# Reordering weight splits around the recurrence chains of a two-layer hybrid decoder, with eight more fill tiles in one wait

## What is computed

```python
p = x @ w_in                                  # (T, 6412): RWKV-7 | retention | mLSTM
o_rw  = rwkv7(...)                            # 8 heads of 64, matrix state, chunks of 128 tokens
o_ret = silu(gr) * rmsnorm(retention(q, k, v))      # 6 heads
o_ml  = sigmoid(om) * rmsnorm(mlstm(q, k, v, i, f)) # 6 heads
mix = concat([o_rw, o_ret, o_ml]) @ w_out
x1 = layernorm(ALPHA * x + mix)
x2 = layernorm(ALPHA * x1 + (silu(x1 @ w_gate) * (x1 @ w_up)) @ w_down)
```

## Time and profile before

| what | value |
|---|---|
| median of 3 runs | 2744.86 us (2743.68 to 2747.96) |
| the profiled execution, its own time | 2746.56 us |
| its span, from the first to the last instruction | 2744.8 us |
| TensorE busy | 2675.2 us, 97% |
| VectorE busy | 1624.7 us, 59% |
| ScalarE busy | 1163.2 us, 42% |
| granted TensorE clock, mean | 0.992 |
| HBM | 433.00 MB read, 162 GB/s |

### The profile page before, as it was taken

One profiled execution on the slowest core, in us unless ns is written; L12 is line 12 of the kernel. 1 busy time (PEld: TensorE's weight loads), 2 busy tenths in 40 slices (PEclk: granted clock), 3 DMA queues, 4 the chain that ended last, 5 costly groups with the idle time before them and its releaser, 6 DMA issues.

```text
span 2744.8 us, 55654 instructions
## 1 busy us (share of the span) xinstructions
PE 2675.2 (97%) x23551; PEld 2619.0 (95%) x23551; DVE 1624.7 (59%) x1768; ACT 1163.2 (42%) x1460; POOL 0.2 (0%) x4
## 2 busy tenths in 40 slices
PE   7999999999999999999999999999999999999997
PEld 7998899999999999999999998988999999999997
DVE  5567457788545455455586574577965555545444
ACT  4445343455333333333364453344643333333332
POOL 0000000000000000000000000000000000000000
PEclk9999999999999999999999999999999999999998
DMA  7644235366655666555565542353766665556653
GB/s 228 189 141 117 86 86 172 108 189 185 177 182 176 184 181 179 177 184 179 183 186 166 179 122 78 86 164 109 199 188 180 176 185 178 183 178 184 208 178 115
DMA packets 280774, 448.98 MB, mean 164 GB/s; under 512 B 45302, under 2 KB 76592, under 8 KB 280312
## 3 DMA queue, kind: packets, MB, share of 16 engines
q1 hardware_dynamic: 278984, 443.21, 54.2%
q10 hardware_dynamic: 1618, 3.24, 0.4%
HBM read 433.00 MB, written 11.78 MB: 162 GB/s over the span
## 4 chain that ended last, share of the span: by engine, by line
PE 87%; DVE 8%; ACT 2%; issue 2%; DMA 1%; ACTq 0%; SPq 0%; DVEq 0%
PE psum L705 19%; PE psum L707 19%; PE psum L706 19%; PE psum L738 6%; PE psum L739 5%; PE psum L740 5%; DVE w_lo L1756 2%; ACT w_hi L1323 1%; PE psum L728 1%; PE psum L729 1%; PE psum L730 1%; PE psum L937 1%; PE psum L1097 1%; PE psum L1082 1%; PE psum L1086 1%
## 5 line engine op out<-in xcount | busy, mean ns | idle before, releaser
L1752 DVE TENSOR_TENSOR w_lo<-w_raw,w_hi 128x1024 fp32r<-128x1024 f32 x496 | 606.1, 1225 | 680.6 <-ACT w_hi L1310 679.5
L1310 ACT ACTIVATE w_hi<-w_raw 128x1024 fp32r<-128x1024 f32 x504 | 533.7, 1060 | 887.0 <-PE psum L707 858.2
L705 PE MATMUL psum<-x_hi,w_lo 128*128 128x264 f32 (+3 forms) x3072 | 877.6, 286 | 2.3 <-DVE x_lo L2081 1.0
L706 PE MATMUL psum<-x_lo,w_hi 128*128 128x264 f32 (+3 forms) x3072 | 874.8, 285 | 0.0
L707 PE MATMUL psum<-x_hi,w_hi 128*128 128x264 f32 (+3 forms) x3072 | 874.3, 285 | 0.0
L705 PEld LDWEIGHTS psum<-x_hi,w_lo 128*128 128x128 f32 x3072 | 579.4, 189 | 3.5 <-issue 1.3
L706 PEld LDWEIGHTS psum<-x_lo,w_hi 128*128 128x128 f32 x3072 | 580.6, 189 | 0.2
L707 PEld LDWEIGHTS psum<-x_hi,w_hi 128*128 128x128 f32 x3072 | 579.5, 189 | 0.0
L1756 DVE TENSOR_TENSOR w_lo<-w_raw,w_hi 128x1024 fp32r<-128x1024 f32 x304 | 367.6, 1222 | 204.1 <-ACT w_hi L1323 187.7
L738 PE MATMUL psum<-x_hi,w_lo 128*128 128x264 f32 (+1 forms) x1376 | 412.0, 299 | 8.4 <-DVE w_lo L1756 5.2
L1323 ACT ACTIVATE w_hi<-w_raw 128x1024 fp32r<-128x1024 f32 x292 | 304.1, 1055 | 269.2 <-PE psum L740 164.8
(11 more groups left out here) (496 smaller groups left out, 2505.6 us busy)
## 6 DMA issues: line engine op xcount, KB each, us to landing
w_raw<-in_w_in SPq DMA_DIRECT2D x192, 512.0 KB, 4.2
w_raw<-in_w_gate SPq DMA_DIRECT2D x176, 512.0 KB, 3.8
w_raw<-in_w_up SPq DMA_DIRECT2D x176, 512.0 KB, 3.9
w_raw<-in_w_down SPq DMA_DIRECT2D x176, 512.0 KB, 3.7
w_raw<-in_w_out SPq DMA_DIRECT2D x64, 512.0 KB, 4.2
w_raw<-in_w_in SPq DMA_DIRECT2D x16, 262.0 KB, 2.8
r_sample<-in_state_ret SPq DMA_DIRECT2D x6, 512.0 KB, 7.7
out_s_ret<-r_sample SPq DMA_DIRECT2D x6, 512.0 KB, 6.2
```

Source lines behind the costliest of these rows:

```text
L705: mm(out, w1, bh[:, k, 0:nt], start=(k == 0), stop=False)
L706: mm(out, w0, bl[:, k, 0:nt], start=False, stop=False)
L1310: A(wh[:, j, :, :], raw[:, j, :, :], ACT.Copy).then_inc(S.hi_ready, 1)
L1752: TT(wl[:, j, :, :], raw[:, j, :, :], wh[:, j, :, :].bitcast(F32), ALU.subtract).then_inc(S.lo_ready, 1)
```

## The change

Five things change, all in the order of the instruction streams. (1) The first layer's plan has 45 instead of 37 tiles ahead of tok0, so that every later step of its RWKV part lies 8 tiles further on; the tiles come off those behind the last step. (2) Goals of the steps named in `waiting` are no longer two slabs behind TensorE: on ScalarE tok, pairs, more and l, on VectorE tok and l, in both chunks and both layers (`name[:-1]` takes the chunk's number off). (3) ScalarE's Tanh and Sigmoid of the gate inputs move from ahead of v0 to behind the squares at syt. (4) In the retention part VectorE makes one split ahead of the second pair, and the others of v1 and v2 behind the third. (5) The scans no longer take a split between them, and the splits of step kks move from ahead of the wait for the spread norm to behind L2222.

```diff
--- before.py
+++ after.py
@@ -474,7 +474,7 @@
     rw_last = [('sa', 16), ('sv', 7), ('sy', 17), ('gn', 5), ('gnss', 8), ('gnsp', 9)]
     rw_steps = [
         [('in', 0), ('a', 7), ('g', 7), ('kk', 11), ('kks', 9), ('bonus', 24)] +
-        chunk_steps(0, 37) + chunk_steps(1, 10) + rw_last,
+        chunk_steps(0, 45) + chunk_steps(1, 10) + rw_last,
         [('in', 0), ('a', 7), ('g', 7), ('kk', 11), ('kks', 9), ('v', 88), ('bonus', 6)] +
         chunk_steps(0, 28) + chunk_steps(1, 12) + rw_last]
     ml_steps = [('spread_m', 14), ('spread_e', 12), ('turn0', 18), ('turn1', 5), ('score', 5), ('num0', 9), ('num1', 7),
@@ -492,11 +492,12 @@
     class Parts:
 
 
-        def __init__(self, plan_, one, pos, slabs=GROUP_SLABS):
+        def __init__(self, plan_, one, pos, slabs=GROUP_SLABS, waiting=()):
             self.i, self.one, self.goals, before = 0, one, {}, 0
             at_ = lambda tile: slab_of(pos, slabs, tile)
             for name, n in plan_.items():
-                self.goals[name] = max(at_(before), at_(n) - 2, at_(max(n - 1, 0)) // slabs * slabs)
+                behind = 0 if name[:-1] in waiting else 2
+                self.goals[name] = max(at_(before), at_(n) - behind, at_(max(n - 1, 0)) // slabs * slabs)
                 before = n
             self.goals['end'] = at_(plan_['end'])
             self.names = list(self.goals)
@@ -1349,7 +1350,7 @@
                                 act.wait_ge(S.a_done, 3 * l + 1)
                             A(pml[:, 4 * (group - 8) + n, :], ps[:, n, 0:T], ACT.Copy).then_inc(S.bank_free, 1)
                     hi_in(l, 8 * pos + RING + i)
-                return Parts(plan_, one, pos)
+                return Parts(plan_, one, pos, waiting=('tok', 'pairs', 'more', 'l'))
 
 
             xp = a['x_prompt'][0].rearrange("(t p) d -> p t d", p=128)
@@ -1440,10 +1441,6 @@
                     bg.to(name)
                 act.wait_ge(S.a_kv_turned, n + 1)
                 A(kst[:, :, :].rearrange("p a k -> p (a k)"), ps[:, 4, 0:128 * AP_], ACT.Copy).then_inc(S.a_kv_ready, 1)
-                if not ml:
-                    act.wait_ge(S.rw_mix, l + 1)
-                    A(px[0:64, 12, 0:T], px[0:64, 12, 0:T], ACT.Tanh)
-                    A(px[:, 13, 0:T], px[:, 13, 0:T], ACT.Sigmoid).then_inc(S.rw_in, 1)
                 for name in tuple(f'v{p}' for p in range(AP_)) + ('sy',):
                     bg.to(name)
                 act.wait_ge(S.a_y_kept, 3 * n + 2)
@@ -1451,6 +1448,9 @@
                 bg.to('syt')
                 A(sq[:, 3:AH, 0:SEQ], ay[:, 3:AH, 0:SEQ], ACT.Square)
                 if not ml:
+                    act.wait_ge(S.rw_mix, l + 1)
+                    A(px[0:64, 12, 0:T], px[0:64, 12, 0:T], ACT.Tanh)
+                    A(px[:, 13, 0:T], px[:, 13, 0:T], ACT.Sigmoid).then_inc(S.rw_in, 1)
                     bg.to('sumsq')
                 act.wait_ge(S.a_y_ready, n + 1)
                 if ml:
@@ -1995,7 +1995,10 @@
                     carried()
                     dve.wait_ge(S.a_sample_loaded, 48 * (n + 1))
                 for p in range(AP_):
-                    bg.to(f'v{p}')
+                    if ml or p == 0:
+                        bg.to(f'v{p}')
+                    if not ml and p == 1:
+                        bg.step()
                     dve.wait_ge(S.a_vspread, n * AP_ + p + 1)
                     b0 = 4 if ml or p != 1 else 6
                     kv = ps[:, b0:b0 + 2, :].rearrange("p a (b v) -> p (a b) v", v=128)
@@ -2004,6 +2007,9 @@
                     else:
                         STT(sam[:, p, :, :], sam[:, p, :, :], gam[:, p:p + 1], kv, ALU.mult, ALU.add).then_inc(S.a_pair_done, 1)
                     dve.wait_ge(S.a_pair_done, n * AP_ + p + 1)
+                if not ml:
+                    bg.to('v1')
+                    bg.to('v2')
                 if ml:
                     carried()
                     dve.wait_ge(S.m_n_loaded, 48 * (l + 1))
@@ -2187,7 +2193,7 @@
                 attention(l, False, 2 * l, bg)
 
 
-                bg = Parts(rw_plan[l], lambda i: lo1(s0 + 8 * RW_POS + RING + i), RW_POS)
+                bg = Parts(rw_plan[l], lambda i: lo1(s0 + 8 * RW_POS + RING + i), RW_POS, waiting=('tok', 'l'))
                 then = (lambda ins: (own(ins), bg.step()))
                 dve.wait_ge(S.bank_free, freed(l, IN_ORDER.index(1)))
                 for i in range(5):
@@ -2200,7 +2206,7 @@
                 for b in range(4):
                     for c in range(NCH):
                         cs = slice(CH * c, CH * c + CH)
-                        then(v.tensor_tensor_scan(lw[:, b, cs], ones, lw[:, b, cs], 0.0, ALU.mult, ALU.add))
+                        own(v.tensor_tensor_scan(lw[:, b, cs], ones, lw[:, b, cs], 0.0, ALU.mult, ALU.add))
                 mid = lw[:, :, 0:SEQ].rearrange("p b (c i) -> p b c i", i=CH)[:, :, :, CH // 2 - 1]
                 own(TS(amid[:, :, :], mid, -DECAY, None, ALU.mult))
                 TS(namid[:, :, :], mid, DECAY, None, ALU.mult).then_inc(S.rw_cum, 1)
@@ -2211,7 +2217,6 @@
                 dve.wait_ge(S.rw_kk_norm, l + 1)
                 invert(RW_HEADS, S.rw_kk_inv)
                 dve.wait_ge(S.rw_kk_raw, l + 1)
-                bg.to('kks')
                 dve.wait_ge(S.rw_kk_spread, l + 1)
                 then(TT(mx[:, 0:4, :], mx[:, 0:4, :], ps[:, 4:8, 0:T], ALU.mult))
 
@@ -2220,6 +2225,7 @@
 
                 then(TT(tmp[:, :, :], px[:, 0:4, 0:T], px[:, 4:8, 0:T], ALU.mult))
                 TT(tmp[:, :, :], tmp[:, :, :], over(cols(l, 'rw_rk', 4), T), ALU.mult).then_inc(S.rw_bonus_in, 1)
+                bg.to('kks')
                 then(TT(mx[:, 4:8, :], mx[:, 4:8, :], mx[:, 0:4, :], ALU.mult))
                 if l:
                     dve.wait_ge(S.bank_free, freed(l, IN_ORDER.index(2)))
```

## The result

The changed kernel takes **2749.8 us**, the median of 22 executions (2744.86 to 2752.64), the kernel before 2745.22 (22 executions, 2742.83 to 2748.61) beside it. The ratio is 1.0014, with a 95% interval of 1.0008 to 1.0019: **some 4 us slower**, within 0.2% and yet outside the range that I gave (2736 to 2749). The forecast was 2742.4.

A forecast was written before the change was run, and what follows sets the result against it. TensorE was taken as the bound, so only its waits and half-clock stretches count. Waits -0.3, stretches gone +5.9, new stretches -3.1: 2.5 us faster, 2742.4 us against the median; range 2736 to 2749.

The forecast's parts named there:

- Sample pairs: Before L937, both layers: a split off the chain and later gate functions save 1.65 of 2.43 us, twice: +3.3.
- Scans and kks: Before L1018, both layers: with the split off the scans, all behind comes 0.8 us sooner, twice: +1.6.
- bonus, first layer: First layer, before L1029: splits leave the chain to L2222, so TensorE's wait of 3.33 us goes: +3.3.
- slabs, second layer: Second layer: moved splits make slabs late, 3.1 us of it behind the wait for group 2's banks: -5.3.
- tok0, first and second: Wait before L1042 falls from 2.48 to 1.6 us in the first layer, +0.9; two more splits in the second, -2.5.
- Pairs, with tile 176: L2280 to L2286: rw_qb waits go, rw_mq waits shrink by 0.9 us, tile 176's bank wait loses 1.3: +2.6.
- End of chunk 0: Behind L2337, both layers: tok1's higher goal takes one more split, waiting for an unfinished slab; 1.8 and 1.5 us: -3.3.
- w1, first layer: First layer: w1's goal takes in split 29, whose slab 33 is loaded late, delaying L1630: -1.7 us.
- clock, over all executions: Four stretches at 1.2 GHz in the recurrence parts go, +5.9 us; two new ones come behind new waits, -3.1.
- the two signs of being wrong: No wait near 1611 us in the second layer, or the half-clock stretches vanish or double.
- The slower one: Rival: each of seven new waits over 1.2 us brings a half-clock stretch, 11.2 us in all, so 2750.5; chance 0.11.
- Nothing: Rival: the order of splits doesn't set the chain, only latencies do; 2744.9 us, chance 0.10.

The follow-up runs named there:

- kks_second: Changed kernel with the kks splits back ahead of the wait for the spread norm in the second layer alone; 2744.74 us, ratio 1.0002 to before.
- kks_first_alone: Kernel before with only the kks splits moved, in the first layer alone; 2740.52 us, ratio 0.9987.
- links_kks: links_only plus the kks splits moved in the first layer alone; 2735.95 us, ratio 0.9967 to the kernel before.
- links_only: Kernel before with splits taken off the sample pairs' links (gate functions behind the squares) and off the scans, both layers; 2740.09 us, ratio 0.9980.
- goals_undone: Changed kernel with every goal two slabs behind TensorE again, order of splits among links kept; 2745.32 us, ratio 1.0001 to before.
- first_only: Kernel before with the whole change made in the first layer alone, 8 tiles included; 2743.5 us, ratio 0.9993.
- no_tok: Changed kernel with only tok's goal two slabs behind again, in both layers; 2745.53 us, ratio 1.0004 to before.

## Why the prediction was wrong

Point by point, in its own steps. A wait is read as the time between the starts of two matmuls less the 0.125 us of dense ones; + is saved.

| step | predicted | profile |
|---|---|---|
| Sample pairs | +3.3 | +2.8 |
| Scans and kks | +1.6 | +1.6 |
| bonus, first layer | +3.3 | +3.3 |
| slabs, first layer | -1.9 | -1.75 |
| slabs, second layer | -5.3 | -3.7 |
| tok0, first and second | +0.9, -2.5 | +0.75, -2.6 |
| Pairs, with tile 176 | +2.6 | **-0.1** |
| l0 | +2.7 | +2.6 |
| End of chunk 0 | -3.3 | -4.1 |
| w1, first layer | -1.7 | -2.4 |
| not foreseen: L1001, second layer | 0 | -0.25 |
| **waits** | **-0.3** | **-3.9** |
| clock, over all executions | +2.8 | **-0.8** |

**Right:** the places. Every new wait named under "To look for" is there: 0.91 before L938, none before L1030, 3.00 on w_lo behind p_rw's banks (I had 3.1), tok0 of the second layer late by 2.6, L1132 late. That rw_qb would be gone from the waits did not come true. Neither of the two signs of being wrong that I had named came up, either: what failed was not among them. `kks_second` shows the second layer's slab waits to come from the kks move, `kks_first_alone` and `links_kks` its use in the first, `links_only` the links.

**Wrong, first step: Pairs.** "The first kind, 2.4 + 0.64, goes: the splits that waited for ScalarE's copies are made before the pairs." It went from L1057 and came back at L1069, the matmul of l behind more, which I had not looked at: 2.17 idle in the second layer. VectorE there, and ScalarE's copy for which it waits:

```profile
1659.64 0.86 DVE L2286 TENSOR_TENSOR rw_tT<-psum,masks 64x256 f32<-64x256 f32 x2
1662.80 1.23 DVE L1756 TENSOR_TENSOR w_lo<-w_raw,w_hi 128x1024 fp32r<-128x1024 f32 x1 [2.29 <-ACT w_hi L1324]
1664.05 0.69 DVE L2288 TENSOR_TENSOR rw_qb<-psum,masks 128x512 f32<-128x512 f32 x1
```

```profile
1661.63 1.06 ACT L1324 ACTIVATE w_hi<-w_raw 128x1024 fp32r<-128x1024 f32 x1 [6.91 <-PE psum L741]
```

A then-step between L2286 and L2288 takes the split of a slab on which TensorE is still at work, and the link waits 2.29 us for it. I had counted the splits due before a piece and not those that a then-step takes within it, although I had seen just that at more1 and at the end of chunk 0. `goals_undone` shows that the goals only moved the wait: there L1069 waits 0.4 in all, and L1058 waits 2.9 on rw_qb again. The term was off by 2.7 of the 3.6 by which the sum of the waits fell short. Of the rest, 0.8 is the end of chunk 0, 0.7 w1, 0.5 the sample pairs (1.4 each, not 1.65), and the second layer's slabs gave 1.6 back: slabs 9 and 10 were not late, and two old waits left, one on a slab near 1619 and one on p_tail near 1629 (0.48 and 0.72). That this miss ran the other way was luck, not foresight. w1's size is its transfer: issued at 387.65 among the state's loads, and ScalarE's copy waits for it until 392.80, 5.1 us for a median of 4.2:

```profile
387.65 0.53 SPq L535 DMA_DIRECT2D w_raw<-in_w_in  x1
```

```profile
392.80 1.06 ACT L1324 ACTIVATE w_hi<-w_raw 128x1024 fp32r<-128x1024 f32 x1 [7.69 <-DMA w_raw<-in_w_in]
393.76 0.58 ACT L1630 ACTIVATE rw_w<-psum 128x512 f32<-128x512 f32 x1
```

The estimate from the Trainium skill's page DMA: Bandwidth & Descriptors (Anatomy of one DMA), 3.2 us, is further off still. The page fits it to transfers that GpSimd issues, while SyncE issues this one, among other loads; which of the two makes the difference no run isolates.

**Wrong, second step: Clock.** "By the spacing in them, the four stretches at 1.2 GHz cost 1.7, 1.7, 1.0 and 1.5, and the idle time ahead of each goes: +5.9." I credited the stretches of one execution as if they were the kernel's. Three of the four were not there in the next two profiles of the same kernel (those at 278.7, 1661.1 and 1671.3), while others were (near 356 and 1513). Taken over all executions, the clock's share is -0.8, not +2.8. Of the four only the one by L1029's wait stands in all three profiles of before, and in all three of the changed kernel one stands behind the new wait of 3.00 on w_lo (1608.6, 1608.8, 1610.7). So the regular stretch of before was traded for a regular one behind the new wait, as my nearest row had said of that one; the other three credits had nothing regular under them. The same holds in the other kernels: each of the 14 waits of 3.0 us or more in the recurrences of the 18 profiles has a half-clock stretch beside it; of the 64 between 1.9 and 2.9 us some four in ten have. The Trainium skill's page TensorE: Matmul & The Clock Gate (Part 1) says that the monitor runs freely; the profiles agree for the shorter waits, whose stretches moved. I had let it widen the range only, where it spoke against a credit of 2.8. Nor are 27 matmuls the most that 3.4 us at full clock hold, as I had read it: at 1671.3 the changed kernel has 64 there, since the chains' matmuls are narrower.

In these parts the profiles of before have 4, 4 and 5 stretches of 3.4 us, those of the changed kernel 1, 2 and 3. That looks like the half that I had forecast, but all three of the latter fell on executions with more clock than the mean (0.994, 0.994 and 0.993 against 0.9923). Without either long wait the mean clock was 0.9939 in `kks_first_alone` and 0.9942 in `links_kks`, but 0.9932 in `first_only` and 0.9926 in `kks_second`, which lack both too. `kks_second`, `no_tok` (0.9922) and the changed kernel (0.9919, 0.9928, 0.9925 by lot) differ by no more than lots of one kernel do. What the changed kernel's other waits cost in clock stays open.

**The rivals.** The slower one (2750.5) gave the right number by the wrong cause: it laid its whole loss to stretches behind seven waits, while 3.1 of the 3.9 us between the means of all executions stay at like clock, and the profiles have 1 to 3 stretches there. "Nothing" fell too: the order of splits does set the chains.

**What stays open:** by the rows of the first pair of profiles the waits cost 3.9 us, at like clock 3.1. That is mostly the choice of profiles. In the first one of before the waits on rw_qb are 2.4, in the two others 3.0; its half-clock stretch at 278.7, just ahead of the pairs, may be why, but no run isolates it:

```profile
PE psum L1057 <- DVE rw_qb L2282: 3.0, 4, 1.4
```

(the third profile of before). The third profile of the changed kernel has 1 us less of waits, and over three profiles of each the difference of all idle time is the 3.0 given above.

## What to carry to other kernels

Work that fills an engine's gaps may stand behind a link of a chain only if its input is there by then: ahead of a wait it costs its duration, but with an input that another engine still makes it costs that engine's lateness too, on the chain. Ask this of each place by itself (the same move gained some 2 to 3 us in one layer and lost 3.7 in the other, where a wait for banks stood behind it), and run the parts alone: two parts of this change are worth 9 us. And take no credit for a clock stretch from one profile; compare executions at like granted clock, which here told 3 us apart where the medians of 11 could barely do so, and price the difference of the mean clocks by itself.

## What the runs showed of the hardware

The granted clock of the changed kernel ranged from 0.990 to 0.994 (44 executions) and that of the kernel before from 0.991 to 0.994 (139), at 1.8 us per 0.001, so some 6 us of spread while the waits of three profiles agree within 1 us in all. In the recurrences a stretch at half clock lasted 3.4 or 6.8 us in every profile. All 14 waits of 3.0 us or more had one, beginning within the wait or up to 1.4 us behind it; behind shorter waits its place moved between executions. The two kernels that took L1029's wait away with nothing added had the highest mean clocks of those that ran 37 tiles, 0.9939 and 0.9942.

A stretch also stands where TensorE did not wait at all: during or right behind 128 matmuls of a single column each (L1169 in before), which take 3.9 us at full clock. It is there in the first layer in all 18 profiles (near 430) and in the second in 17 (near 1800). One such group in the first profile of before, and TensorE's stretch behind it:

```profile
1799.75 3.90 PE L1169 MATMUL psum<-p_rw,rw_sample 64*64 64x1 f32 x128
```

```profile
1804.40:1807.80 3.40, 3.40 (x15) 0.51 0.24 34
```
